# Folding a 32-token tile, splitting MLA scores into high/low products and reordering the units of an attention stage, on one core

## What is computed

```python
def sb_attend(q, k, v, t0):                       # layer A: 16 heads of 64, strictly causal
    z = einsum('bqhd,bkhd->bhqk', q, k) * SB_HEAD_DIM ** -0.5
    log_stay = where(mask, log_sigmoid(-z), 0.0)
    after = cumsum(log_stay, axis=3, reverse=True) - log_stay
    w = where(mask, exp(log_sigmoid(z) + after), 0.0)
    return einsum('bhqk,bkhd->bqhd', w, v)

def mla_attend(q, k_nope, k_pe, v, t0):           # layer B: 8 heads, 128 + 64 rotary, v 128
    s = (einsum('bqhd,bkhd->bhqk', q[..., :128], k_nope)
         + einsum('bqhr,bkr->bhqk', q[..., 128:], k_pe)) * 192 ** -0.5
    p = softmax(where(chunk mask, s, NEG_BIG))    # chunks of 64 frames
    return einsum('bhqk,bkhd->bqhd', p, v)

# layer A:  x = x + (silu(gate) * attend(q, k, v)) @ w_o      q, k RMS-normed per head
# between:  latent (512) and rotary key (64) from x, normed; k_nope, v = latent @ w_kv_b
# layer B:  x = x + (silu(gate) * attend(q, k_nope, k_pe, v)) @ w_o_b,  q = norm(x @ w_in) @ w_q_b
# y = rms_norm(x); outputs: y, new k and v of layer A, latent and rotary key, prompt and sample
```

## Time and profile before

| | us |
|---|---|
| median of 3 runs | 852.7 (851.94 to 853.42) |
| the profiled execution: its own time | 846.55 |
| its span, first to last instruction | 844.7 |
| TensorE busy | 800.8 (95%) |
| VectorE busy | 451.9 (53%) |
| ScalarE busy | 331.0 (39%) |
| GpSimd busy | 314.6 (37%) |
| mean granted TensorE clock | 0.991 of full speed |

### The profile page before, as it was taken

How to read it: one execution, slowest core, us unless ns; L and a number is a source line. 1 busy time by engine, 2 the same in 40 slices (tenths; PEclk the granted TensorE clock), 3 DMA queues, 4 the chain that set the end, 5 groups by cost and what they waited for, 6 DMA issues and landing times.

```text
span 844.7 us, 13543 instructions
## 1 busy us (share of the span) xinstructions
PE 800.8 (95%) x4623; PEld 654.1 (77%) x4623; DVE 451.9 (53%) x1023; ACT 331.0 (39%) x840; POOL 314.6 (37%) x261
## 2 busy tenths in 40 slices
PE   5799999999999999988999899999999999999996
PEld 4688888878887878756878878998777777765785
DVE  5556666666767585874146432116755555656222
ACT  6444334333333333442177332324444343446211
POOL 5345252534344343551313453445433233333100
PEclk9899999999999999999999999999999999999999
DMA  7631303030303030313223142321102011020211
GB/s 212 159 102 47 87 29 106 26 109 25 107 25 107 25 107 25 101 47 113 79 87 111 69 146 75 88 88 45 44 23 66 1 41 59 26 96 5 106 50 57
DMA packets 68082, 61.68 MB, mean 73 GB/s; under 512 B 7144, under 2 KB 55040, under 8 KB 68032
## 3 DMA queue, kind: packets, MB, share of 16 engines
q1 hardware_dynamic: 68032, 61.04, 23.6%
HBM read 50.85 MB, written 10.17 MB: 72 GB/s over the span
## 4 chain that ended last, share of the span: by engine, by line
PE 87%; DVE 5%; ACT 3%; SPq 1%; issue 1%; POOL 1%; DMA 1%; POOLq 0%; ACTq 0%; DVEq 0%
PE bank L428 17%; PE bank L430 16%; PE bank L429 16%; PE bank L688 5%; PE bank L722 3%; PE bank L995 3%; PE bank L700 3%; PE bank L1039 2%; PE bank L1041 2%; PE bank L1040 2%; PE bank L1023 2%; PE bank L993 2%; PE bank L758 2%; PE bank L760 2%; PE bank L759 2%; PE bank L972 1%
## 5 line engine op out<-in xcount | busy, mean ns | idle before, releaser
L1506 POOL TENSOR_TENSOR wlo<-raw,whi 128x1024 fp32r<-128x1024 f32 (+3 forms) x80 | 194.8, 2443 | 116.8 <-ACT whi L1125 116.5
L428 PE MATMUL bank<-whi,hthi 128*128 128x384 f32 (+1 forms) x360 | 129.5, 360 | 2.5 <-DVE wlo L1717 2.3
L430 PE MATMUL bank<-whi,htlo 128*128 128x384 f32 (+1 forms) x360 | 126.1, 350 | 0.0
L429 PE MATMUL bank<-wlo,hthi 128*128 128x384 f32 (+1 forms) x360 | 126.0, 350 | 0.0
L1125 ACT ACTIVATE whi<-raw 128x1024 fp32r<-128x1024 f32 (+3 forms) x84 | 82.4, 1007 | 24.8 <-PE bank L760 20.6
L1780 DVE TENSOR_TENSOR_SCAN left<-stay 128x512 f32<-128x512 f32 (+4 forms) x72 | 70.8, 983 | 18.8 <-ACT stay L1217 18.5
L1569 POOL TENSOR_TENSOR rstd<-msq,neg_half 128x4 f32<-128x4 f32 x40 | 40.3, 1007 | 98.4 <-DVE msq L1747 97.6
L428 PE MATMUL bank<-hthi,whi 128*128 128x272 f32 x256 | 75.0, 293 | 0.0
L428 PEld LDWEIGHTS bank<-whi,hthi 128*128 128x128 f32 x360 | 69.7, 194 | 6.6 <-issue 5.1
L430 PE MATMUL bank<-hthi,wlo 128*128 128x272 f32 x256 | 73.6, 287 | 0.0
L429 PE MATMUL bank<-htlo,whi 128*128 128x272 f32 x256 | 73.4, 287 | 0.0
(11 more groups left out here) (202 smaller groups left out, 1749.4 us busy)
## 6 DMA issues: line engine op xcount, KB each, us to landing
raw<-in_w_in_a SPq DMA_DIRECT2D x64, 256.0 KB, 3.1
raw<-in_w_in_b SPq DMA_DIRECT2D x24, 256.0 KB, 3.2
...
```

Source lines behind the costliest of these rows:

```text
L428: eng.matmul(dst, st[0], mv[0], start=(k == 0), stop=False)
L429: eng.matmul(dst, st[0], mv[1], start=False, stop=False)
L430: mm = eng.matmul(dst, st[1], mv[0], start=False, stop=(k == n - 1))
L1506: nc.gpsimd.tensor_tensor(wlo[slot][:, c], raw[:, c], whi[slot][:, c].bitcast(F32), ALU.subtract).then_inc(s_lo, 1)
```

## The change

Five things are changed together.

1. **The sample tile is folded.** The high operand gets 32 more columns per block of 128 rows (`HS` = 576), and the sample's low part lies there. Two passes (`two`) then give high by high and high by low in rows 0 to 31, and low by high (with low by low) in rows 32 to 63; the rows 32 to 63 are added to the first ones. In stage A that is a new step "L" (ScalarE copies 32 x 384, VectorE adds); in the products with w_o_a and w_o_b it is a second addition on VectorE. The projections of latent, query and gates are not folded.
2. **`wgt` is gone.** The weights of stage A are written over `stay`, and ScalarE's next write to it waits for the transposes.
3. **The MLA scores of the prompt** are five fp32r passes (qh by kh, qh by kl, ql by kh, qr by kpeh, qr by kpel) and the mask. `qr` holds high and low of the rotary query in its two halves of the partitions. The low parts are made by VectorE (`xlo_d`) out of `XB`, which stays taken until that is done (`s_xlo2`). For token tile 0 the passes are 128 columns wide.
4. **Stage D goes by token tile**, both heads of tile 3, then of tile 2 and so on, with one buffer for the queries, the sums in five steps O, and new orders of chunks and steps. "V" is the transpose of any chunk (before, "X" and "Y").
5. **The last product** takes tiles 3, 2, 1, 0 and the sample, in five banks; 24 of its steps (each of 3 passes) lie in `LAST_D`, 14 before.

The diff, cut to its core:

```diff
-STEP_D = [("Q", 0), ("P", 5), ("N", 0), ("K", 0), ("S", 0), ("N", 1), ("R", 0), ("Q", 1), ("X", 0), ("S", 1),
...
+CHUNKS = [("K", 0), ("K", 1), ("Q", 3), ("K", 2), ("Q", 2), ("K", 3), ("Q", 1), ("K", NT), ("Q", NT), ("K", TT), ("Q", 0)]
+          ("C", 5), ("T", 3), ("R", 4), ("N", 5), ("S", 5), ("V", 4), ("C", 6), ("T", 4), ("R", 5), ("N", 6), ("V", 5),
...
+        def two(eng, dst, pairs):
+            n = len(pairs)
+            for k, (st, mv) in enumerate(pairs):
+                eng.matmul(dst, st, mv[0], start=(k == 0), stop=False)
+                mm = eng.matmul(dst, st, mv[1], start=False, stop=(k == n - 1))
+            return mm
...
@@ proj_a, TensorE @@
+                if c == NT:
+                    two(pe, b[:, 0:3 * P], [(acol(ht[0], k, c, HS), w[k]) for k in range(KD)]).then_inc(s_proj, 1)
+                    return
...
@@ ScalarE @@
+            def fold_a(q, par, c):
+                act.wait_ge(s_proj, CA * q + c + 1)
+                act.wait_ge(s_normed, TT * q + c)
+                nc.scalar.activation(fold[:, :], PRJ[(par + c) % 2][SMP:2 * SMP, 0:3 * P], ACT.Copy).then_inc(s_fold, 1)
@@ VectorE @@
+            def fold_a(q, par, c):
+                dve.wait_ge(s_fold, q + 1)
+                b = PRJ[(par + c) % 2][0:SMP, 0:3 * P]
+                v.tensor_tensor(b, b, fold[:, :], ALU.add).then_inc(s_folded, 1)
...
-                v.tensor_tensor(wgt[0:r, ub, 0:n], left[0:r, ub, SEQ - n + 1:SEQ + 1], left[0:r, ub, SEQ - n:SEQ],
+                v.tensor_tensor(here, left[0:r, ub, SEQ - n + 1:SEQ + 1], left[0:r, ub, SEQ - n:SEQ],
                                 ALU.subtract).then_inc(s_wgt, 1)
...
@@ turn_qk, TensorE @@
                 if begun(CD * q + c):
                     pe.wait_ge(s_xev2, CD * q + c)
+                if begun(LD * q + lows(c)):
+                    pe.wait_ge(s_xlo2, LD * q + lows(c))
...
@@ score_d, TensorE @@
-                pe.matmul(b[:, 0:(i + 1) * P], q2t[:, par, h, i * P:(i + 1) * P], k2t[:, par, h, 0:(i + 1) * P],
-                          start=True, stop=False)
-                pe.matmul(b[:, 0:(i + 1) * P], q2t[r, par, 2, i * P:(i + 1) * P], kpet[r, 0:(i + 1) * P],
-                          start=False, stop=True)
+                pe.matmul(dst, qh[:, h, tile], kh[:, par, h, 0:n], start=True, stop=False)
+                pe.matmul(dst, qh[:, h, tile], kl[:, par, h, 0:n], start=False, stop=False)
+                pe.matmul(dst, ql[:, h, tile], kh[:, par, h, 0:n], start=False, stop=False)
+                pe.matmul(dst, qr[:, h, tile], kpeh[:, 0:n], start=False, stop=False)
+                pe.matmul(dst, qr[:, h, tile], kpel[:, 0:n], start=False, stop=True)
...
@@ VectorE @@
+            def xlo_d(q, par, c):
+                what, t = CHUNKS[c]
+                if t >= NT:
+                    return
+                tile = slice(t * P, (t + 1) * P)
+                dve.wait_ge(s_xev2, CD * q + c + 1)
+                nope = XB[:, 0:2 * P].rearrange("p (m c) -> p m c", m=2)
+                if what == "K":
+                    v.tensor_tensor(kl[:, par, :, tile], nope, kh[:, par, :, tile].bitcast(F32),
+                                    ALU.subtract).then_inc(s_xlo2, 1)
+                    return
+                v.tensor_tensor(ql[:, :, tile], nope, qh[:, :, tile].bitcast(F32), ALU.subtract)
+                for h in range(2):
+                    own = slice(h * ROPE, (h + 1) * ROPE)
+                    other = slice((1 - h) * ROPE, (2 - h) * ROPE)
+                    last = v.tensor_tensor(qr[other, h, tile], XB[own, 2 * P:3 * P], qr[own, h, tile].bitcast(F32),
+                                           ALU.subtract)
+                last.then_inc(s_xlo2, 1)
...
@@ last_product, TensorE @@
-                pe.matmul(b, st[0], mv[1], start=False, stop=False)
-                return pe.matmul(b, st[1], mv[0], start=False, stop=(k == KD - 1))
+                mm = pe.matmul(b, st[0], mv[1], start=False, stop=(t == NT and k == KD - 1))
+                if t < NT:
+                    mm = pe.matmul(b, st[1], mv[0], start=False, stop=(k == KD - 1))
```

517 lines of the change are left out of this document (320 added, 197 removed), and 27 rows, old and new, of tables (LAST_D, STEP_A, STEP_D).

## The result

The changed kernel takes 899.35 us (median of 4 runs, 894.28 to 901.36), the kernel before 852.32 on the same chip (4 runs, 850.49 to 853.42). The ratio on record is 1.0534, 95% interval 1.0481 to 1.0588 (the two medians divided give 1.055): slower by 47 us. The direction was forecast, the size was not: 872 was said, with 885 as the upper end.

What follows compares the result with a forecast made beforehand. TensorE was taken to set the pace; 34 us less work would be outweighed by waits on other engines: 18.5 + 1.2 − 1.4 + 0.6 = 18.9, plus 1 for the clock, so 852.7 + 20, said as 872; range 858 to 885.

Steps and rivals of the forecast that it cites:

- The chain through `XB`: Stage D: split, power, norm, maximum, exponential, copies and low parts in series take 12.0 us beside 9.45 of TensorE work.
- The first rival: Whole kernel: chains stay hidden, needing 9.5 us instead of 12.0, so TensorE keeps its pace: 822 to 835; chance 0.08.
- the term for the clock: Whole kernel: 1 us added to the sum of 18.9 for the granted clock, making +20.
- The clock falls behind the waits: Rival, some 15 waits: half bring 2 us at clock 0.50, at most +7 above forecast, 879; chance 0.2.
- stage D with the end: Steps +14.1, pair 2's splits +1.2, `FILL_D` +3.7, `LAST_D` +3.2, sample group of the end −3.7: +18.5 us.
- front and pairs of stage A: Stage A: the fold keeps only −0.9, its copy and addition cost +2.1: sum +1.2 us, bounds −10 and +7.
- middle: Product with w_o_a: saves 3.7 us, 2.3 of it lost to waits: −1.4, bounds −3.7 and +1.
- tail: Tail of the kernel: one more addition of 32 x 512, +0.6 us.
- So of 11.2 us only the fill keeps its part, −0.9: Stage A: folding saves 11.2 us of passes, which turn into TensorE waits on VectorE except −0.9 in the fill.
- T6's unit sees 0.3 in each of seven steps: +2.1: Stage A: new copy and addition lengthen chunk 4's chain by about 1 us, 0.3 of it felt per step.
- The place of `wgt` in `stay` costs nothing: Stage A: writing weights in place is free while ScalarE is early; otherwise each of 72 units could lose 0.1.
- TensorE's busy time down by about 34 us: Sign in the changed profile: TensorE's work falls by 11.2 + 3.7 + 3.7 + 15 us, its share near 89%.

Runs made afterwards that it cites:

- e2: Changed kernel with unread TensorE passes added inside four kinds of waits in stage D (three per step, one in the last pair): 889.47 us, ratio 1.0454.
- e1: Changed kernel with each weight split moved behind the next projection chunk at four places of STEP_D: 873.66 us, ratio 1.0251.
- e13: Changed kernel with new stage D orders, pair 0 not folded, idle time in stage A's last pair filled, GpSimd's second split late: 831.73 us, ratio 0.9748.
- e7: Changed kernel with 13 and 22 unread passes filling two idle stretches of the last pair of stage A: 894.28 us, ratio 1.0468.
- e3: Changed kernel with the sample tile of stage A unfolded, in its own passes at its old place in STEP_A: 897.55 us, ratio 1.0528.
- e11: Changed kernel with a 128 x 1 GpSimd subtraction ahead of the second low split of every stage A pair: 895.54 us, ratio 1.0572.
- e5: Kernel before with only the stage A weights written in place into `stay`, `wgt` removed: 847.91 us, ratio 0.9945.
- e8: Changed kernel with STEP_D and LAST_D laid out anew and value products waiting for the whole sum ahead: 858.53 us, ratio 1.0079.

## Why the prediction was wrong, and what in it held

**It held: the mechanism of the waits and its place.** The chain through `XB` is in the trace in the order that was written down; what it left out is the mean that is held beside the split. The single waits, of which the clock is no part:

| wait | predicted | measured |
|---|---|---|
| V3 | 3.2 | 2.9 |
| V5 | 2.5 | 1.5 |
| V7 | 2.5 | 2.9 |
| V9, with O4 behind it | 1.0 | 0.3 |
| P, last step | 3.0 | 2.9 |

A step of 61.5 with 10.2 us at half clock would have been at least 56.4 at full clock, where 56.9 was said; e2 and e1 show independently that clock and chain are two parts. The first rival (TensorE keeps its pace) fell: it needed a chain of 9.5 us. e1 meets its main condition, that the power does not wait behind the split, and a step still takes 53.2, with waits of 1.0 to 1.6.

**Failed: the term for the clock.** The step that failed reads "and 1 us for the clock (below)", and behind it the rival "The clock falls behind the waits", with "a us each at most, +7", at a chance of 0.2. The changed kernel has 77 us more at half clock, at most 39 us of time. The stretch of 2 us that the rival reckoned with has no row: the fall of the earlier trace rows itself goes on to 488.3 and lasts 6.8 us, as the next window of before shows.

```profile
485.00:488.00 3.00, 3.00 (x16) 3.00 (x16) 0.17 (x1) 0.98 (x3) 2.36 (x1) 0.50 0.28 98
```

All eight waits of 2.9 us or more in stage D (V3 and V7 of three steps, P, and one of 3.6 at an end product) are followed by 3.4 or 6.8 us at half clock, not 2; of the waits of 1.5 us at V5 none is, and of the four of 1.4 to 1.7 in `FILL_D` one. The terms of the sum against the trace (profiled executions, "clock" being half of the added time at half clock, an upper bound):

| term | predicted | measured | of it clock, at most |
|---|---|---|---|
| stage D with the end | +18.5 | +38.9 | 20.4 |
| front and pairs of stage A | +1.2 | +9.8 | 5.1 |
| middle | −1.4 | +4.6 | 11.9 |
| tail | +0.6 | +0.7 | 1.1 |

Without the clock stage D is at +18.5 or more, where +18.5 was said. That the two figures agree is luck, since within it errors cancel: the waits at V5 and V9 are smaller, and `FILL_D` lost 5.6 for 3.7, since its waits are 1.4 to 1.7 and not 0.8 to 1.1. The prediction's own figures also slip a little: eight heads at 5.5 less 3.7 are 14.4 us and not 15. In the middle the bound is looser than the cost: with the same products and no half clock (e13) the stretch from the first early product to the latents takes 99.4, before it took 102.6, and the changed kernel 106.65. So the product with w_o_a kept 3.2 of its saving, and 7.2 us went to idle time and the clock behind it. That the clock fell there at all was in no term. Idle time has a part in it (e7), but the kernel before has waits of 1.2, 1.8 and 2.6 us in its last pair of stage A without a fall, where the changed one has 17.1 us at half clock behind a wait of 1.45. What makes the difference is open.

**Failed, small: two places of stage A.** "So of 11.2 us only the fill keeps its part, −0.9": the front got 3.6 longer (and an eighth of 11.2 is 1.4, not 0.9). Folding makes the first pair's fifth tile wait for a chain (2.54 us at `qkr`), and 3.4 us more are at half clock; e3 takes it back to 59.9. And "T6's unit sees 0.3 in each of seven steps: +2.1": the pairs lost 6.2. One pair has a fall of the clock (6.8 us at half) and takes 45.8, some 1.7 more than the others. Of the rest, part is the scan that takes 3.46 for 1.22: e11 takes off some half a microsecond a pair that has no fall. "The place of `wgt` in `stay` costs nothing" held (e5). That the folded tile's passes gain little in stage A held too (e3).

**The narrow passes.** Taken as 0.21 for 128 columns and 0.12 for 256, bounds 0.06 and 0.42. The changed kernel shows 0.11 and 0.12, start to start, the 128-column ones here:

```profile
667.04 0.28 PE L1076 MATMUL bank<-kl,qh 128*128 128x128 f32 x1
667.15 0.28 PE L1077 MATMUL bank<-kh,ql 128*128 128x128 f32 x1
667.26 0.27 PE L1078 MATMUL bank<-kpeh,qr 128*128 128x128 f32 x1
```

For 128 columns the price was too high, and the waits hid the difference.

**"TensorE's busy time down by about 34 us"** failed for the same reason as the total: passes at half clock count nearly double. In e1, with a clock of 0.967, it is 791.9, in e13 779.3. A share near 89% was said and 90% came, out of a busy time and a span that were both wrong.

So the change loses by the order of its steps. Its saving in passes is real; e8's steps and e13's total show it once no chain through `XB` is longer than TensorE's work beside it.
